# The order of the first loads: x ahead of the vectors and the first modulation weights

## The reference, cut to what matters

```
c_lat = silu(c);  c_con = silu(c_ctx)
mod_l = split(c_lat @ ada_w[i] + ada_b[i], 6)      # 1024 x 6144 weights per layer
mod_c = split(c_con @ ada_w[i] + ada_b[i], 6)
h_lat = rmsnorm(x,   norm_mix_g[i]) * (1 + mod_l[1]) + mod_l[0]
h_ctx = rmsnorm(ctx, norm_mix_g[i]) * (1 + mod_c[1]) + mod_c[0]
```

## Time and profile before

| what | value |
|---|---|
| median of three runs | 3304.5 us (3299.94 to 3307.04) |
| the profiled execution | 3305.98 us |
| its span, first to last instruction | 3303.9 us |
| TensorE busy | 2764.6 us, 84% of the span |
| VectorE, ScalarE, GpSimd busy | 815.1, 407.3, 231.3 us |
| granted TensorE clock, mean | 0.924 |
| first stage ends (last VectorE instruction) | 41.63 us |
| first large matmul (L388) starts | 59.68 us |

### The profile page before, as it was taken

The page is one execution under the profiler, slowest core; times in us unless marked ns, Lnnn a source line. Parts: engine busy times, 40 slices in busy tenths (PEclk is TensorE's granted clock), DMA queues, the critical chain, the costliest instruction groups (busy, mean ns, idle before and its releaser), DMA issues. The chain is left out here.

```text
span 3303.9 us, 30779 instructions
## 1 busy us (share of the span) xinstructions
PE 2764.6 (84%) x12976; PEld 1347.7 (41%) x12976; DVE 815.1 (25%) x1391; ACT 407.3 (12%) x716; POOL 231.3 (7%) x206
## 2 busy tenths in 40 slices
PE   4999897759999994999888587777658767899999
PEld 2585465424444442467333222222223543344444
DVE  2514485230000002011672300000131764100100
ACT  2001341110000002000150200000011131110000
POOL 1000000100101012000001000000112000000000
PEclk8999898979999996999999799999879867899999
DMA  5230112369999992233400899999712100121211
GB/s 220 114 141 28 48 32 89 143 241 389 390 394 396 390 388 72 115 140 115 120 0 26 334 395 400 400 399 401 289 51 78 53 0 26 64 89 63 98 62 68
DMA packets 91115, 599.99 MB, mean 182 GB/s; under 512 B 10472, under 2 KB 13880, under 8 KB 29680
## 3 DMA queue, kind: packets, MB, share of 16 engines
q1 hardware_dynamic: 76960, 527.89, 40.7%
q0 software_dynamic: 12880, 68.23, 6.6%
q10 hardware_dynamic: 1152, 2.10, 0.2%
HBM read 570.85 MB, written 23.13 MB: 180 GB/s over the span
## 5 line engine op out<-in xcount | busy, mean ns | idle before, releaser
L752 PE MATMUL moe_psg<-moe_ring,moe_xs 128*64 128x512 f32 x1024 | 253.3, 637 | 39.8 <-DMA moe_ring<-in_experts 37.5
L752 PE MATMUL moe_psu<-moe_ring,moe_xs 128*64 128x512 f32 x1024 | 236.0, 599 | 32.2 <-DMA moe_ring<-in_experts 31.8
L752 PE MATMUL moe_psd<-moe_ring,moe_hid_t 128*64 128x512 f32 x1024 | 237.7, 602 | 30.2 <-DMA moe_ring<-in_experts 28.5
L914 DVE TENSOR_SCALAR moe_y_l<-moe_psd,moe_gates 128x512 f32<-128x512 f32 x32 | 24.0, 751 | 643.9 <-PE moe_psh L766 331.6
L388 PE MATMUL ffg_ps<-h_feat,feed_f_slots 128*128 128x512 f32 x352 | 153.3, 598 | 10.2 <-ACTq L406 10.2
L388 PE MATMUL ffd_ps<-ff,feed_f_slots 128*128 128x512 f32 x352 | 151.3, 592 | 1.4 <-DVEq L406 1.4
L388 PE MATMUL ffu_ps<-h_feat,feed_f_slots 128*128 128x512 f32 x352 | 151.3, 592 | 1.3 <-DVEq L406 1.3
L752 PEld LDWEIGHTS moe_psg<-moe_ring,moe_xs 128*64 128x64 f32 x1024 | 73.1, 144 | 190.4 <-issue 161.5
L752 PEld LDWEIGHTS moe_psd<-moe_ring,moe_hid_t 128*64 128x64 f32 x1024 | 68.5, 137 | 190.7 <-issue 128.9
L752 PEld LDWEIGHTS moe_psu<-moe_ring,moe_xs 128*64 128x64 f32 x1024 | 67.0, 136 | 179.3 <-issue 110.8
L766 PE MATMUL moe_psgu<-moe_ring,moe_xs 128*32 128x256 f32 x2048 | 117.1, 380 | 0.0
(11 more groups left out here) (415 smaller groups left out, 3396.6 us busy)
## 6 DMA issues: line engine op xcount, KB each, us to landing
moe_ring<-in_experts SPq DMA_DIRECT2D x384, 1024.0 KB, 18.9
feed_f_slots<-in_ffn_gate SPq DMA_DIRECT2D x11, 1024.0 KB, 4.8
feed_f_slots<-in_ffn_up SPq DMA_DIRECT2D x11, 1024.0 KB, 4.8
feed_f_slots<-in_ffn_down SPq DMA_DIRECT2D x8, 1408.0 KB, 6.5
mod_ada_w<-in_ada_w SPq DMA_DIRECT2D x2, 4096.0 KB, 13.4
qk_ada_w<-in_ada_w POOLq DMA_DIRECT2D x2, 4096.0 KB, 14.9
v_ada_w<-in_ada_w POOLq DMA_DIRECT2D x2, 4096.0 KB, 14.7
mout_ada_w<-in_ada_w POOLq DMA_DIRECT2D x2, 4096.0 KB, 13.1
```

The source lines that it names most:

```text
L752: mm = pe.matmul(ps_lat[part][64 * half:64 * half + 64, :], lhs, ring[:, n % SLOTS, m, half * HALF:(half + 1) * HALF], start=(k == 0), sto ...
L914: ins = dve.tensor_scalar(y_l[:], ps_lat[DOWN][:], gates[:, 0, e, :], None, ALU.mult)
```

## The change

SP issues the load of x first; vec, ident and the first modulation weights follow. The four loads are the same, on the same queue, and so are their semaphores and all waits.

```
--- before
+++ after
@@ first_stage, block.sync @@
             def _(sp):
+                sp.dma_start(K.x[:], dram["x"]).then_inc(sig["x"], 16)
                 sp.dma_start(K.vec[:, :, 0], dram["vec"]).then_inc(sig["vec"], 16)
                 sp.dma_start(K.ident[:], dram["ident"]).then_inc(sig["ident"], 16)
                 mods.load(sp, 0, 1)
-                sp.dma_start(K.x[:], dram["x"]).then_inc(sig["x"], 16)
                 mods.load(sp, 1, 2)
                 prefetch(sp)
```

## The result

The changed kernel takes 3310.29 us (median of 20 runs, 3308.05 to 3314.89), the kernel before 3305.55 (20 runs, 3299.94 to 3310.43). The ratio is 1.0015 with a 95% interval of 1.0008 to 1.0022, so 3 to 7 us slower. The forecast was 3310.6, as +6.1 us on 3304.5; the difference of the medians is +4.7. The profiled execution took 3313.97 us, span 3311.9.

A forecast was written before the change was run, and what follows sets the result against it. The first stage was taken as bound by the chain load, product, load, product, evacuation. Terms 6.4 - 0.3 + 0 = +6.1 us on a median of 3304.5 gave 3310.6 us, range 3305.5 to 3315.0.

The forecast's parts named there:

- Order of the transfers: SP's queue at the start: whatever is issued ahead is paid in full by what stands behind; upper bound +7.3 us.
- First ada_w, +6.4: First modulation weights, now last of four loads, land at 22.6 us: x's old landing 23.45 less 0.87; bounds +5.5 to +7.3.
- The 0.87 us: Pause of the DMA engines at 21.0 to 22.0 us, behind SP's second ada_w issue; taken away after the change.
- The lower bound: First ada_w's landing: 7.59 MB moved by 21.5 us, 0.08 MB left, so nothing lands before 21.7, +5.5.
- Second ada_w, -0.3: Second modulation load, issued into an empty queue, takes 12.1 us from issue to landing instead of 12.4; bounds -1.3 to +0.6.
- The two products, 0: TensorE's two first-stage products keep their sum of 4.94 and 6.42 us, +-1.5, though the clock's turns are open.
- vec, the squares, the feed, priced at 0: First stage: later vec is hidden, squares and sums gain 11 us unused, feed chunks have 21 us of cover; 0.
- Rival 1: End of the queue and products: order costs its full price, pause belongs to the last transfer; +8.2 us, 3312.7; 25%.
- Rival 2: Short tail: first ada_w lands at 21.7, second 11.1 us after issue; +4.2 us, 3308.7; 10%.
- Rival 3: Order at issue doesn't matter: engines take both big loads side by side, TensorE starts at 16.2; +0, 3304.5; 11%.
- rival 4: Later stages: granted clock's falls move and give the time back, 12.7 us, to some 3297; 4%.
- the forecast's own +-3.2: Range from landing +-0.9, second load +-0.8, products +-1.5 and median of runs +-2: 3307.4 to 3313.8 us.

The follow-up runs named there:

- vec_then_x: Kernel before with only x moved ahead of the first ada_w, vec and ident still in front: 3313.6 us, ratio 1.0022.
- x_waits: Kernel before with one wait more, SP issuing the second ada_w only when x has landed: 3306.0 us, ratio 1.0000.
- warm_after: Changed kernel with TensorE kept busy before both products by matmuls that nothing reads: 3309.7 us, ratio 1.0012 to the kernel before.
- x_last: Kernel before with x issued behind the second ada_w: 3319.0 us, ratio 1.0042.
- two_before: Kernel before with the second ada_w issued at once, without the wait, into a second place (qk and o): 3302.2 us, ratio 0.9995.
- ada_first: Kernel before with the first ada_w issued in front of vec and ident, x last: 3303.3 us, ratio 0.9992.
- best: Kernel before with first ada_w in front, second issued at once into a second place, TensorE kept busy by idle matmuls: 3303.1 us, ratio 0.9995.

## Why the prediction was right, and where it was not

The forecast hit the time (3310.6 against 3310.29) and the direction. As an effect it was +6.1 against +4.7 by the medians, +5.0 by the ratio and +5.45 by the trace.

- *Order of the transfers.* Right. x in front delays what is behind it by its bytes: vec_then_x, which moves x alone, has its first product 7.1 us later (23.30 - 16.18), against 7.3 forecast as the upper bound.
- *First ada_w, +6.4.* It was +5.33, outside the bounds (5.5 to 7.3), and this is the step that failed. The 0.87 us were read as standing engines and laid to SP's next issue. The packet records show rows under way all through them, and x_waits and vec_then_x show that the late end has nothing to do with the issue: without it the end still comes at 23.3. What the change spared, 1.8 to 2.0 us, came from vec no longer being in front, an edit that the prediction had priced at nothing. A wrong reason took away half of the right amount, and that the time came so close is in part luck. The lower bound failed as well: 7.59 MB are what had started by 21.5 in the kernel before, with three engines behind, and this was taken as given for the new order.
- *Second ada_w, -0.3.* 27.80 to 40.01 is 12.2; right within 0.1.
- *The two products, 0.* 6.24 + 5.53 = 11.77 against 11.36: +0.4, inside +-1.5. Over the kernels without idle matmuls single products took 4.9 to 6.5 us; that TensorE's idling is the cause was shown by warm_after. The prediction took the two values of one execution as agreeing with a difference from run to run; the runs show that difference directly: the same first product, started at 15.8 to 16.2, took 4.94 (before), 5.62 (x_last), 5.75 (x_waits) and 6.48 us (two_before).
- *vec, the squares, the feed, priced at 0.* The squares gained 12 us that nothing used, as forecast, and the first large matmul waited 16.21 us on the same barrier as before. For the landing vec was not worth 0: this is where the missing 1 us of the first step lies.
- *Sum of the stage.* +5.33 + 1.30 - 0.28 - 0.89 = +5.46 (landing, first product, second load, second product), as the first large matmul shows.
- *Rivals.* Rival 1's premise (the late end is the loads' own) was right, but its price didn't come due, because another edit of the same change removed it. Rival 2 had the landing nearly right (21.7) for no reason that held, and the second load wrong (11.1 against 12.2). The Trainium skill's fit for GpSimd's path (DMA: Bandwidth & Descriptors, Anatomy of one DMA) gives 20.4 for the four, an estimate; the changed kernel was 1.1 us later than that, and the quickest order (ada_first, 21.20) 0.8. Rival 3 is refuted by vec_then_x. Of rival 4's kind was the rest of the profiled execution, 2.6 us against the change; the medians don't show it.
- *Range.* The four parts of the forecast's own +-3.2 (0.9, 0.8, 1.5, 2) give 2.8 when added in squares; this changes nothing in the outcome.

Open is why a quarter megabyte of small rows in front leaves some engines behind. Four profiles with vec in front lie at 23.15 to 23.52, and eight others at 21.20 to 22.53, which makes chance unlikely; but two of these (warm_after, best) also had a late end of 1 us, both with TensorE kept busy. There it was a single step of the 16 (22.38 behind 21.56, and 22.51 behind 21.19). Whether that is cause or chance wasn't tried.

## What to carry to other kernels

When loads share a queue, ask of each not only who waits for it but which later load waits for that waiter: here 5 us came from a 4 MB load that was issued late, while the DMA engines stood empty. Another place for it took 9.0 us off the changed order but 0.6 off the order of before, where x's bytes fill the wait: such a place pays where the engines would stand empty. An operand moved forward gains only if its own chain was late; its slack (3.2 us here) can be read beforehand. When a stall is laid to a neighbour in time, look for a second place where the same stall stands without this neighbour, and ask what the view counts: a window with no new packets isn't one without packets.

## What was not expected of the hardware

- The same 7.67 MB landed about 1.8 us later with 257 KB of 2 KB rows in front (23.15 to 23.52) than with a large load in front (21.20 to 21.71 where TensorE idled). Three to five of the 16 steps of the load's semaphore were late, from the first large load behind vec on. 64 KB of 512-byte rows in front did little (21.86).
- Small loads on a second queue were not fast: 257 KB took 13.4 us and 64 KB 20.4 us to land beside 7 MB on the other queue, against 2.8 us for vec at the head of the one queue that held all loads.
- The view of the granted clock reads 1.00 in the first product of the kernel before and of the changed kernel, though its matmuls run at the pace of the lower level for 2.5 and 5.4 us. For the kernel before this is in the earlier trace rows; a window of the changed kernel:

```profile
21.51:26.90 5.39, 5.39 (x52) 2.88 (x56) 0.00 (x0) 1.22 (x2) 4.95 (x3) 1.00 0.00 0
```

  52 matmuls in 5.39 us are the pace of the window at 0.50 (1.2 GHz) in the earlier trace rows. The trace's first clock record stands at 18.83 in the kernel before and at 26.78 in the changed one, which is where the pace turns; the 1.00 ahead of it is no reading. There the pace of the matmuls has to be read.
